# A two-layer attention network and two expert layers on one core: the order of the first transfers, the order of the first norms, and ten blank products

## The chip, the cores and the metric

The kernel runs on one core of one Trainium2 chip. The metric is the device time of one execution in microseconds (us); less is better. A core has TensorE (PE in the profile; PEld is its loading of weights), VectorE (DVE), ScalarE (ACT), GpSimd (POOL) and SyncE (SP). Each engine works through its own list of instructions in order and waits on semaphores for the others. Transfers are issued here by SP and, a few, by ACT; they run on 16 DMA engines that both queues share.

## The reference, cut to what matters

256 tokens of width 1024 pass through a first block of two layers (each with its own attention and an attention to 256 memory tokens) and then through a second block of two layers with three kinds of attention and 16 experts. The change touches only the beginning of the first layer:

```python
h = rmsnorm(x, norm_g[0])                    # rows x rsqrt(mean square) x a gain for each column
mem_h = rmsnorm(mem, mem_norm_g[0])
proj = einsum('bsd,de->bse', h, w_in_a[0])   # q, k, v of 24 heads, memory query, gate
kv = einsum('bnd,de->bne', mem_h, w_kv)      # keys and values of the memory, 4 heads
k = rmsnorm(k_of(kv), mem_kn_g[0])           # norm of each memory key over its 128 numbers
o_mem = softmax(q_mem @ k.T) @ v_of(kv)
```

## The kernel before, in words

**Products.** All large products are made from pairs of float32r numbers. A weight is cut into a high part (ACT, line 440) and what is left of it (DVE, line 448), and an activation likewise; a product is then three TensorE instructions (lines 507 to 509: high with high, low weight with high, high with low). The weights are walked in *quarters* of 256 rows of a 512-column slab: quarter q goes through ring buffer, ACT's cut, DVE's cut and TensorE's step q. A step is 2 token tiles x 2 blocks of 128 rows x 3 instructions = 12 products of 512 columns. Five cut quarters can be held at once (`NQ`), so ACT's cut of quarter q waits for TensorE's step q - 5.

**The first steps.** Steps 0 to 3 make the memory's keys (slab `mk0`), steps 4 to 7 its values (`mv0`); step 8 is the first quarter of `a00`, the first projection of the layer's own rows. The activations are not transposed on the chip: `mem_turned` and `x_turned` come turned from memory, ACT multiplies them by the norm's gain column by column and rounds to the high part (`act_gain_high`, line 697), DVE makes the low part (`dve_gain_low`, line 704). The row factors of the norm (`act_rows_norm`, line 730, and `dve_rows_factor`) are applied later, when ACT moves a finished product out of its bank (`act_proj_out`, line 575).

**The order around the change** is written out by hand in `act_layer_a`, `dve_layer_a`, `pe_layer_a` and `sp_first`:

- ACT issues two small transfers (`act_first_loads`): `gcol`, the gain columns (48 numbers on each of 128 partitions), and the first part of `const`, which holds the identity matrix. Both count on the semaphore `d_id`, and ACT and DVE begin with a wait for both (32).
- ACT then makes mhT (the memory's rows) with the cuts of quarters 0 to 2 between its pairs, cuts quarter 3, squares `mem_rows`, cuts quarters 4, 5 and 6 and moves `mk0` out; then come the norm of the memory keys (`act_head_norm`: squares at line 751, quarter 7, a root, quarter 8), and after it the eight instructions of hT (the layer's own rows), quarters 9 and 10, and so on.
- DVE follows the same order: `dve_head_norm` is quarter 7, the sum at line 763, the root (717 to 721), quarter 8, a multiplication (766), quarter 9, and the gain (771), which also needs `rows`; then the eight low parts of hT.
- TensorE does steps 0 to 8, turns the normed memory keys (`pe_flip`, line 656), and goes on with step 9.
- SP issues, in this order: half of `mem_turned`, half of the first ring load, the other half of `mem_turned`, ring loads to 2, `mem_rows`, ring load 3, `rows` (gains of the head norms), `x_turned`, ring load 4, `x_rows`, ring load 5, the rest of `const`. A ring load past the third waits until the buffer's last quarter has been cut by DVE.

Of the kernel before, what the change touches and what calls it, by code (L numbers as in the profile page):

```python
# [125 lines left out]
def program(nc, t, out, cols, keep):  # L126
# [14 lines left out]
    def sb(name, *shape, at=None, dt=F32):  # L141
        size = 4
        for n in shape[1:]:
            size *= n
        if at is None:
            place[name] = top_of[0]
            top_of[0] += (size + 63) // 64 * 64
        else:
            place[name] = place[at[0]] + at[1]
        return nc.alloc_sbuf_tensor_at(name, list(shape), dt, offset=place[name])  # L150

    def sem(name):
        return ctx.enter_context(nc.semaphore(name))
# [47 lines left out]
    maskR = sb("maskR", P, 2, TOK, dt=F32R)  # L201
    identR = sb("identR", P, P, dt=F32R)
    zeroR = sb("zeroR", P, 1, dt=F32R)
    squares = sb("squares", P, D, at=("S", 0))
    middle = [sb("middle0", P, D, at=("S", 4096)), sb("middle1", P, D, at=("PT", 0))]
    mem_rows = sb("mem_rows", P, 2, D, at=("PT", 0))
# [66 lines left out]
    def R(name):  # L273
        a, b = row_at[name]
        return rows[:, a:b]
# [102 lines left out]
    w_landed = [sem(f"w_landed{i}") for i in range(NR)]  # L378
    w_high, w_low, w_used = sem("w_high"), sem("w_low"), sem("w_used")
    d_id, d_const, d_rows, d_x, d_out = sem("d_id"), sem("d_const"), sem("d_rows"), sem("d_x"), sem("d_out")  # L380
    d_x0, d_x_turned, d_mem_rows, d_first = sem("d_x0"), sem("d_x_turned"), sem("d_mem_rows"), sem("d_first")


    first_normed, first_turned, second_normed = sem("first_normed"), sem("first_turned"), sem("second_normed")
# [15 lines left out]
    def write(pe, act, dve, pool, sp, branch):  # L400
# [12 lines left out]
        def sp_load(until):  # L413
            while sp.q < min(until, len(halves)):
                h = sp.q
                sp.q += 1
                view, srcs = halves[h]
                i = ring_of[h]
                if ring_before[h] >= 0:
                    sp.wait_ge((w_low, 2 * ring_before[h] + 2))  # L420
                for l in range(2):
                    if i >= NS and more_places[l][0] <= h < more_places[l][0] + NR:
                        sp.wait_ge(at("kS", l, 0))
                dst, a = view(ring[i]), 0
                if h == 0:
                    sp.e.dma_start(dst[:, 2:4, :], srcs[0][:, 2:4, :]).then_inc(w_landed[i], 16)
                    continue
                for src in srcs:
                    n = src.shape[2]
                    sp.e.dma_start(dst[:, :, a:a + n], src).then_inc(w_landed[i], 16)  # L430
                    a += n
# [146 lines left out]
        def kept(name):  # L578
            return at("kept", name, 1)
# [146 lines left out]
        def act_rows_norm(key, src, sq, *ready):  # L726
            ss = small(2, "ss", *key)
            for i in range(2):
                act.wait_ge(ready[min(i, len(ready) - 1)])
                act.e.activation(sq[:, i, :], src[:, i, :], SQUARE, accum_out=ss[:, i:i + 1]).then_inc(*act.did("sum", *key))  # L730
            act_root(key, ss, 2, 1.0 / D, "eps6")
# [7 lines left out]
        def dve_rows_factor(key):  # L739
            dve.wait_ge(at("sum", *key))  # L740
            dve_root(key, small(2, "ss", *key), 2, 1.0 / D, "eps6", factor(key))
# [344 lines left out]
        def sp_first():  # L1086
            quarter = 2 * TOK * 2

            def mem_half(n):
                sp.e.dma_start(mem_turned[:, 4 * n:4 * n + 4, :], t["mem_turned"][:, quarter * n:quarter * (n + 1)].rearrange("p (k n) -> p k n", k=4)).then_inc(d_mem[n], 16)  # L1090

            mem_half(0)
            view, srcs = halves[0]
            sp.e.dma_start(view(ring[ring_of[0]])[:, 0:2, :], srcs[0][:, 0:2, :]).then_inc(d_first, 16)
            mem_half(1)
            sp_load(3)
            sp.e.dma_start(mem_rows[:, :, :], t["mem"][0].rearrange("(t p) d -> p t d", p=P)).then_inc(d_mem_rows, 16)
            sp_load(4)
            sp.e.dma_start(rows[:, 0:t["rows"].shape[1]], t["rows"]).then_inc(d_rows, 16)
            sp.e.dma_start(x_turned[:, :, :], t["x_turned"].rearrange("p (k n) -> p k n", k=8)).then_inc(d_x_turned, 16)  # L1100
            sp_load(5)
            sp.e.dma_start(x_rows[:, :, :], t["x_rows"].rearrange("p (t d) -> p t d", t=2)).then_inc(d_x0, 16)
            sp_load(6)
            sp.e.dma_start(const[:, keep:t["const"].shape[1]], t["const"][:, keep:]).then_inc(d_const, 16)
            sp_load(8)
            sp.e.dma_start(X[:, :, :], t["x"][0].rearrange("(t p) d -> p t d", p=P)).then_inc(d_x, 16)
            sp_load((start("o00") + 14) // 2)
            sp.wait_ge(at("values", ("A", 5, 1)))
            for n in range(2):
                mem_half(n)  # L1110

        def act_first_loads():
            act.e.dma_start(gcol[:, :], t["columns"]).then_inc(d_id, 16)
            act.e.dma_start(const[:, 0:keep], t["const"][:, 0:keep]).then_inc(d_id, 16)

        def act_late_loads():
            act.wait_ge(at("tables", "cB"))
# [21 lines left out]
        LINE = [("a12", "g00"), ("a22", "g01"), ("a32", None), ("a42", None), ("a52", "g02"), (None, None)]  # L1139

        def pe_layer_a():
            pe_upto("a02")
            pe_ahead(9)
            pe.wait_ge((d_id, 32))
            pe_flip(("mKT", 0), chunk(qkv[1][1]), 4, [at("heads", "mk", 0)])
            pe_to("a02")
            for u in range(6):
                first, more = LINE[u]
                if first:
                    pe_upto(first)  # L1150
                pe_head_norm()
                if u == 5:
                    pe_ahead(1)
                    pe_gated("o0", 0, OUT_ORDER)
                    pe_upto("o00", 4)
                    pe_ahead(2)
                else:
                    pe_head_norm()
                pe_flip(("qT", u), chunk(qkv[u % 2][0]), 4, [at("heads", "q", u)])
                pe_ahead(2 if u == 5 else 3)  # L1160
                pe_flip(("kT", u), chunk(qkv[u % 2][1]), 4, [at("heads", "k", u)])
                units = group_units(u)
                if more:
                    pe_upto(more)
                if u == 4:
                    pe_to("mq0")
                    pe_head_norm(rope=False)

                    def between(n):
                        if n == 1:  # L1170
                            pe_flip(("qTm", 0), chunk(qkv[0][0]), 4, [at("heads", "mq", 0)])
                        pe_ahead(1 - n % 2)

                    pe_run(units + mem_units(0), between)
                    pe_to("a52")
                elif u == 5:
                    pe_gated("o0", 2, OUT_ORDER)
                    pe_upto("o00", 8)
                    pe_run(units, lambda n: pe_ahead(1 if n in (0, 2, 3) else 0))
                    pe_ahead(1)  # L1180
                    pe_gated("o0", 1, OUT_ORDER)
                    pe_upto("o00", 12)
                else:
                    pe_run(units, lambda n: pe_ahead(1 - n % 2))
                    pe_to(first)

        def act_layer_a():
            act.wait_ge((d_id, 32))
            act_gain_high(("mhT", 0), mem_turned, mhT[0], gcol[:, 16:24], [(d_mem[0], 16), (d_mem[1], 16)], lambda j0: act_cut(j0 // 2))
            act_upto("mv0")  # L1190
            act_ahead(1)
            act_rows_norm(("mem", 0), mem_rows, mem_rows, (d_mem_rows, 16))
            act_ahead(3)
            act_upto("a02")
            act_head_norm(("mk", 0), qkv[1][1], kept("mk0"), [], rope=False)
            act_gain_high(("hT", "A"), x_turned, hT[0], gcol[:, 0:8], [(d_x_turned, 16)] * 2)
            act_ahead(2)
            act_rows_norm(("x", 0), x_rows, mem_rows, (d_x0, 16))
            act_ahead(1)
# [60 lines left out]
                    act_to(first)  # L1260

        def dve_layer_a():
            dve.wait_ge((d_id, 32))
            dve.e.tensor_copy(identR[:, :], ident).then_inc(*dve.did())
            dve.e.tensor_scalar(zeroR[:, :], ident[:, 0:1], 0.0, None, MUL).then_inc(*dve.did("identR"))
            dve_gain_low(("mhT", 0), mem_turned, mhT, gcol[:, 16:24], lambda j0: dve_cut(j0 // 2))
            dve_upto("mv0")
            dve_ahead(1)
            dve_rows_factor(("mem", 0))
            dve_ahead(3)  # L1270
            dve_upto("a02")
            dve_head_norm(("mk", 0), qkv[1][1], gain=R("mk0"), amid=lambda: dve_ahead(1))
            dve_gain_low(("hT", "A"), x_turned, hT, gcol[:, 0:8])
            dve_ahead(1)
            dve_rows_factor(("x", 0))
            dve_ahead(1)
# [1241 lines left out]

            branch(l, lambda: way("few", (dve_few, act_few, pe_few)), lambda: way("all", (dve_all, act_all, pe_all)))

        act_first_loads()
        sp_first()
        dve_layer_a()
        dve_layer_b()
# [65 lines left out]
```

## Time and profile before

| | us |
|---|---|
| median of 3 runs | 1124.66 (1122.42 to 1126.36) |
| the profiled execution | 1124.96 |
| its span, first to last instruction | 1123.6 |
| PE busy | 1063.6 (95%) |
| DVE busy | 885.9 (79%) |
| ACT busy | 743.1 (66%) |

The span is what the profile's records cover; the profiled execution's own time is 1.36 us longer. The granted TensorE clock was 0.982 of full speed on average. "Idle before" in a timeline row stands in square brackets, with what ended it.

### The profile page before, as it was taken

The page shows a single profiled execution, that of the slowest core. Times are in us where ns is not written, and L with a number is a line of the kernel's source. Part 1 is how long each engine was busy: PE and PEld are TensorE (multiplying, and loading weights), DVE is VectorE, ACT ScalarE, POOL GpSimd, SP SyncE. Part 2 cuts the span into 40 slices and gives each one's busy share as a digit, 9 for nine tenths or more (in the row PEclk, how much of TensorE's full clock was granted, in tenths as well). Part 3 has the DMA queues.
Part 4 walks back from the last instruction along what each step waited for, and adds up shares of the span by engine and source line. Part 5 has one row for each costly group of instructions (what it writes and reads, how often), then busy time and mean ns, then how long its engine had stood idle before and what let it go on. Part 6 is the DMA issues. An engine that isn't in the chain of part 4 may idle for free.

```text
span 1123.6 us, 14563 instructions
## 1 busy us (share of the span) xinstructions
PE 1063.6 (95%) x5466; PEld 917.0 (82%) x5466; DVE 885.9 (79%) x1472; ACT 743.1 (66%) x1318; POOL 0.2 (0%) x4
## 2 busy tenths in 40 slices
PE   6899999999998999999999999999989999999996
PEld 5788888888787888888978788888878878788885
DVE  5756857777768867767588779999976877899996
ACT  6646665655666666486555457998845646699993
POOL 0000000000000000000000000000000000000000
PEclk9899999999999999999999899999999989999998
DMA  9754455443433645725542417999936332499991
GB/s 356 270 185 148 150 188 173 160 154 113 159 141 114 212 164 186 237 75 171 170 148 76 150 65 228 364 368 376 344 106 212 113 113 76 151 364 369 384 377 42
DMA packets 131283, 223.36 MB, mean 199 GB/s; under 512 B 6016, under 2 KB 76416, under 8 KB 130944
## 3 DMA queue, kind: packets, MB, share of 16 engines
q1 hardware_dynamic: 127312, 215.31, 55.3%
q10 hardware_dynamic: 3888, 6.98, 2.0%
q8 instruction: 47, 0.77, 0.3%
q14 instruction: 36, 0.29, 0.1%
HBM read 221.23 MB, written 1.05 MB: 198 GB/s over the span
## 4 chain that ended last, share of the span: by engine, by line
PE 48%; DVE 32%; ACT 11%; issue 6%; DMA 1%; SPq 0%; ACTq 0%; DVEq 0%
DVE wL L448 14%; PE bank L507 12%; PE bank L508 11%; PE bank L509 11%; ACT wH L440 4%; PE bank L886 3%; PE bank L822 3%; DVE sm L763 1%; PE bank L871 1%; DVE qkv L766 1%; ACT S L845 1%; DMA mem_rows<-in_mem 1%; PE bank L2302 1%; DVE mx L833 1%; DVE ys L2469 1%
## 5 line engine op out<-in xcount | busy, mean ns | idle before, releaser
L448 DVE TENSOR_TENSOR wL<-ring,wH 128x1024 fp32r<-128x1024 f32 (+1 forms) x316 | 375.3, 1212 | 122.7 <-ACT wH L440 121.9
L440 ACT ACTIVATE wH<-ring 128x1024 fp32r<-128x1024 f32 (+1 forms) x316 | 319.8, 1045 | 24.3 <-PE bank L509 16.3
L507 PE MATMUL bank<-wH,hTH 128*128 128x512 f32 (+2 forms) x592 | 231.2, 391 | 8.8 <-DVE hTL L704 4.4
L508 PE MATMUL bank<-wL,hTH 128*128 128x512 f32 (+2 forms) x592 | 224.3, 379 | 0.0
L509 PE MATMUL bank<-wH,hTL 128*128 128x512 f32 (+2 forms) x592 | 224.1, 379 | 0.0
L507 PEld LDWEIGHTS bank<-wH,hTH 128*128 128x128 f32 x592 | 113.3, 191 | 26.8 <-DVE wL L448 7.3
L509 PEld LDWEIGHTS bank<-wH,hTL 128*128 128x128 f32 x592 | 113.2, 191 | 14.5
L508 PEld LDWEIGHTS bank<-wL,hTH 128*128 128x128 f32 x592 | 113.5, 192 | 13.4 <-issue 0.5
L507 PE MATMUL bank<-wH,xgH 128*128 128x512 f32 x256 | 102.0, 398 | 2.5 <-DVE wL L448 2.3
L508 PE MATMUL bank<-wL,xgH 128*128 128x512 f32 x256 | 97.5, 381 | 0.0
L509 PE MATMUL bank<-wH,xgL 128*128 128x512 f32 x256 | 97.5, 381 | 0.0
L845 ACT ACTIVATE S<-bank,sm 128x256 f32<-128x256 f32 (+1 forms) x144 | 59.7, 428 | 45.0 <-DVE sm L837 42.7
L507 PEld LDWEIGHTS bank<-wH,xgH 128*128 128x128 f32 x256 | 48.8, 191 | 14.6 <-DVE wL L448 7.3
L877 ACT ACTIVATE PT<-bank 128x512 f32<-128x512 f32 x56 | 31.2, 597 | 41.1 <-PE bank L871 41.1
L509 PEld LDWEIGHTS bank<-wH,xgL 128*128 128x128 f32 x256 | 48.7, 190 | 7.0
L508 PEld LDWEIGHTS bank<-wL,xgH 128*128 128x128 f32 x256 | 48.9, 191 | 5.3
L575 ACT ACTIVATE qkv<-bank,factors 128x512 f32<-128x512 f32 x50 | 33.0, 688 | 27.0 <-PE bank L509 27.0
L448 DVE TENSOR_TENSOR wL<-ring_G,wH 128x1024 fp32r<-128x1024 f32 x40 | 48.4, 1218 | 1.0 <-ACT wH L440 1.0
L507 PE MATMUL bank<-wH,gh 128*128 128x512 f32 x128 | 49.0, 383 | 0.0
L448 DVE TENSOR_TENSOR wL<-ring_K,wH 128x1024 fp32r<-128x1024 f32 x40 | 48.2, 1219 | 0.8 <-ACT wH L440 0.7
L508 PE MATMUL bank<-wL,gh 128*128 128x512 f32 x128 | 48.5, 379 | 0.0
L509 PE MATMUL bank<-wH,gh 128*128 128x512 f32 x128 | 48.5, 379 | 0.0
(291 smaller groups left out, 1842.6 us busy)
## 6 DMA issues: line engine op xcount, KB each, us to landing
ring<-in_w_in_a SPq DMA_DIRECT2D x44, 1024.0 KB, 5.1
ring<-in_w_out SPq DMA_DIRECT2D x20, 1024.0 KB, 4.9
ring<-in_w_down SPq DMA_DIRECT2D x20, 1024.0 KB, 7.2
ring<-in_w_gate SPq DMA_DIRECT2D x36, 512.0 KB, 5.6
ring<-in_w_up SPq DMA_DIRECT2D x36, 512.0 KB, 7.2
ring<-in_w_in_b SPq DMA_DIRECT2D x14, 1024.0 KB, 5.2
ring<-in_w_in SPq DMA_DIRECT2D x8, 1024.0 KB, 5.2
ring<-in_w_mem_kv SPq DMA_DIRECT2D x7, 1024.0 KB, 7.2
```

The lines of the kernel that those rows point to most:

```text
L440: act.e.activation(quarter_parts(q)[0], quarter_in_ring(q), COPY).then_inc(w_high, 1)
L448: dve.e.tensor_tensor(lo, quarter_in_ring(q), hi.bitcast(F32), SUB).then_inc(w_low, 1)
L507: pe.e.matmul(o, a[0], high, start=first, stop=False)
L508: pe.e.matmul(o, a[0], low, start=False, stop=False)
L509: return pe.e.matmul(o, a[1], high, start=False, stop=last)
L575: act.e.activation(two_halves(dst(i)), from_woven(bank_of["proj", name, i].t, slab_w[name]), COPY, scale=factor(key)[:, i:i + 1] if key el ...
L763: dve.follow().tensor_reduce(ss.rearrange("p (t h) -> p t h", t=2), sq.rearrange("p t (h d) -> p t h d", d=P), AX, ADD).then_inc(*dve.did( ...
L766: dve.follow().tensor_tensor(v, v, bc(r.rearrange("p (t h) -> p t h", t=2).unsqueeze(3), [P, 2, n, P]), MUL).then_inc(*dve.did())
L822: mm = pe.e.matmul(score_bank(u, s // each)[:, s % each, :], u.qh(s)[:, i * P:(i + 1) * P], u.kh(s)[:, k:k + n], start=u.mask is None, sto ...
L845: act.e.activation(u.S[:, s, 0:n], score_bank(u, s // each)[:, s % each, :], EXP, bias=nb[:, s:s + 1], scale=u.scale, accum_out=u.den[:, s ...
L877: act.e.activation(u.PT[:, kt, :, :].rearrange("p h q -> p (h q)"), bank_of["turn", u.name, kt].t[:, :], COPY).then_inc(*act.did("PT", u.n ...
L886: mm = pe.e.matmul(b.t[:, s * u.dv:(s + 1) * u.dv], u.PT[:, kt, s, :], u.vh(s, kt), start=kt + s == 0, stop=kt == u.nk - 1, skip_group_che ...
```

## The change

1. SP issues `gcol` first of all, on a semaphore of its own (`d_columns`). The first part of `const` goes to SP too, behind ring load 2 and ahead of `mem_rows`, and counts alone on `d_id` (16). ACT issues neither. `x_turned` is issued ahead of ring load 4 as before, and `rows`, which stood ahead of `x_turned`, now comes behind ring load 4.
2. ACT begins with a wait for `d_columns`, and waits for `d_id` only ahead of the squares of `mem_rows`; DVE makes `identR` and `zeroR` there too.
3. On ACT and DVE the eight instructions of hT move ahead of the norm of the memory keys.
4. DVE first clears a new column, `blank`, and TensorE begins with ten products of it with itself, 512 columns each, in plain float32.

```diff
@@ program
+    blank = sb("blank", P, 1)
@@ sp_first
+            sp.e.dma_start(gcol[:, :], t["columns"]).then_inc(d_columns, 16)
             mem_half(0)
             view, srcs = halves[0]
             sp.e.dma_start(view(ring[ring_of[0]])[:, 0:2, :], srcs[0][:, 0:2, :]).then_inc(d_first, 16)
             mem_half(1)
             sp_load(3)
+            sp.e.dma_start(const[:, 0:keep], t["const"][:, 0:keep]).then_inc(d_id, 16)
             sp.e.dma_start(mem_rows[:, :, :], ...).then_inc(d_mem_rows, 16)
             sp_load(4)
-            sp.e.dma_start(rows[:, 0:t["rows"].shape[1]], t["rows"]).then_inc(d_rows, 16)
             sp.e.dma_start(x_turned[:, :, :], ...).then_inc(d_x_turned, 16)
             sp_load(5)
+            sp.e.dma_start(rows[:, 0:t["rows"].shape[1]], t["rows"]).then_inc(d_rows, 16)
             sp.e.dma_start(x_rows[:, :, :], ...).then_inc(d_x0, 16)
-        def act_first_loads():
-            act.e.dma_start(gcol[:, :], t["columns"]).then_inc(d_id, 16)
-            act.e.dma_start(const[:, 0:keep], t["const"][:, 0:keep]).then_inc(d_id, 16)
@@ pe_layer_a
+            pe.wait_ge(at("blank"))
+            b = att_bank(("idle", "first"), None)
+            for _ in range(10):
+                pe.e.matmul(b.t[:, :], blank[:, 0:1].to_broadcast([P, P]), bc(blank[:, 0:1], [P, 512]), start=True, stop=True)
             pe_upto("a02")
             pe_ahead(9)
-            pe.wait_ge((d_id, 32))
+            pe.wait_ge((d_id, 16))
@@ act_layer_a
-            act.wait_ge((d_id, 32))
+            act.wait_ge((d_columns, 16))
             act_gain_high(("mhT", 0), ...)
             act_upto("mv0")
             act_ahead(1)
+            act.wait_ge((d_id, 16))
             act_rows_norm(("mem", 0), mem_rows, mem_rows, (d_mem_rows, 16))
             act_ahead(3)
             act_upto("a02")
+            act_gain_high(("hT", "A"), x_turned, hT[0], gcol[:, 0:8], [(d_x_turned, 16)] * 2)
             act_head_norm(("mk", 0), qkv[1][1], kept("mk0"), [], rope=False)
-            act_gain_high(("hT", "A"), x_turned, hT[0], gcol[:, 0:8], [(d_x_turned, 16)] * 2)
             act_ahead(2)
@@ dve_layer_a
-            dve.wait_ge((d_id, 32))
-            dve.e.tensor_copy(identR[:, :], ident).then_inc(*dve.did())
-            dve.e.tensor_scalar(zeroR[:, :], ident[:, 0:1], 0.0, None, MUL).then_inc(*dve.did("identR"))
+            dve.e.memset(blank[:, :], 0.0).then_inc(*dve.did("blank"))
             dve_gain_low(("mhT", 0), ...)
             dve_upto("mv0")
             dve_ahead(1)
+            dve.wait_ge((d_id, 16))
+            dve.e.tensor_copy(identR[:, :], ident).then_inc(*dve.did())
+            dve.e.tensor_scalar(zeroR[:, :], ident[:, 0:1], 0.0, None, MUL).then_inc(*dve.did("identR"))
             dve_rows_factor(("mem", 0))
             dve_ahead(3)
             dve_upto("a02")
+            dve_gain_low(("hT", "A"), x_turned, hT, gcol[:, 0:8])
             dve_head_norm(("mk", 0), qkv[1][1], gain=R("mk0"), amid=lambda: dve_ahead(1))
-            dve_gain_low(("hT", "A"), x_turned, hT, gcol[:, 0:8])
             dve_ahead(1)
```

## Rows read from the trace of the kernel before

**Rows 1.** Page, part 4: shares of the whole span's chain by engine.

```profile
PE 48%; DVE 32%; ACT 11%; issue 6%; DMA 1%; SPq 0%; ACTq 0%; DVEq 0%
```

**Rows 2.** Waits of PE, 0 to 80 us: total, times, longest.

```profile
PE bank L507 <- DVE wL L448: 10.1, 1, 10.1
PE bank L507 <- DVE hTL L704: 4.4, 1, 4.4
```

**Rows 3.** Windows: length, busy PE, PEld, DVE, ACT, POOL, clock, DMA share, GB/s.

```profile
10.00:15.00 5.00, 4.94 (x12) 3.96 (x13) 4.18 (x8) 4.13 (x7) 0.00 (x0) 1.00 1.06 397
15.00:33.40 18.40, 18.40 (x86) 15.84 (x84) 11.32 (x18) 13.52 (x25) 0.00 (x0) 1.00 1.04 412
37.80:42.30 4.50, 4.46 (x11) 3.58 (x12) 4.32 (x12) 2.33 (x5) 0.00 (x0) 0.50 1.03 405
44.00:72.00 28.00, 28.00 (x131) 24.52 (x130) 13.99 (x15) 14.82 (x17) 0.00 (x0) 1.00 0.66 224
```

**Rows 4.** Chain of waits, 0 to 80 us: start, length, what.

```profile
4.26 13.39 DMA mem_rows<-in_mem
...
24.45 1.06 ACT T L751
...
30.37 3.20 ACT hTH L697 x8
...
35.69 1.22 DVE qkv L771
...
42.88 0.87 PE bank L656 x8
```

**Rows 5.** Timeline of ACT, the first waits: start, length, operation.

```profile
6.89 0.91 ACT L697 ACTIVATE mhTH<-mem_turned,gcol 128x256 fp32r<-128x256 f32 x2 [4.88 <-DMA const<-in_const]
17.68 1.06 ACT L730 ACTIVATE mem_rows<-mem_rows 128x1024 f32<-128x1024 f32 x1 [2.33 <-DMA mem_rows<-in_mem]
```

**Rows 6.** Timeline of DVE, 26 to 36 us: cuts of quarters 7, 8, 9.

```profile
26.49 1.23 DVE L448 TENSOR_TENSOR wL<-ring,wH 128x1024 fp32r<-128x1024 f32 x1 [1.58 <-ACT wH L440]
...
30.40 1.23 DVE L448 TENSOR_TENSOR wL<-ring,wH 128x1024 fp32r<-128x1024 f32 x1 [0.38 <-ACT wH L440]
...
34.54 1.23 DVE L448 TENSOR_TENSOR wL<-ring,wH 128x1024 fp32r<-128x1024 f32 x1 [1.78 <-ACT wH L440]
```

**Rows 7.** DMA issues: queue, size, us from issue to landing.

```profile
x_turned<-in_x_turned SPq DMA_DIRECT2D x1, 1024.0 KB, 11.6
rows<-in_rows SPq DMA_DIRECT2D x1, 776.0 KB, 9.7
```

**Rows 8.** Timeline of the issuing queues: start and length of an issue.

```profile
0.76 0.39 ACTq L1113 DMA_DIRECT2D gcol<-in_columns  x1
...
13.11 0.43 SPq L1100 DMA_DIRECT2D x_turned<-in_x_turned  x1
```

**Rows 9.** Windows of the first transfers; last number GB/s.

```profile
4.00:6.00 2.00, 0.00 (x0) 0.00 (x0) 0.00 (x0) 0.00 (x0) 0.00 (x0) 1.00 0.83 224
6.00:8.00 2.00, 0.00 (x0) 0.00 (x0) 0.46 (x3) 1.11 (x3) 0.00 (x0) 1.00 1.04 413
```

**Rows 10.** Timeline of PE: two plain float32 products of 512 columns.

```profile
860.07 1.88 PE L1763 MATMUL bank<-wukv,mKT 128*128 128x512 f32 x4
```

**Rows 11.** Timeline of PE and windows (PE busy, clock): products with a zero column.

```profile
666.02 2.87 PE L516 MATMUL bank<-zeroR,identR 128*128 128x512 f32 x12
...
664.00:668.00 4.00, 4.00 (x28) 1.00 0.01 2
```

**Rows 12.** Timeline of PE and the windows around it: short gaps, clock after.

```profile
624.86 0.66 PE L975 MATMUL bank<-const,Y 128*128 128x128 f32 x4 [1.23 <-DVE Y L893]
...
626.00:632.00 6.00, 6.00 (x16) 0.50 1.02 330
...
370.77 0.45 PE L507 MATMUL bank<-wH,yTH 128*128 128x512 f32 x1 [1.07 <-DVE yTL L992]
...
371.00:374.00 3.00, 3.00 (x15) 1.00 0.75 289
```

More of the change, by code:

```diff
@@ L380, in program @@
     d_id, d_const, d_rows, d_x, d_out = sem("d_id"), sem("d_const"), sem("d_rows"), sem("d_x"), sem("d_out")
-    d_x0, d_x_turned, d_mem_rows, d_first = sem("d_x0"), sem("d_x_turned"), sem("d_mem_rows"), sem("d_first")
+    d_x0, d_x_turned, d_mem_rows, d_first, d_columns = sem("d_x0"), sem("d_x_turned"), sem("d_mem_rows"), sem("d_first"), sem("d_columns")
     first_normed, first_turned, second_normed = sem("first_normed"), sem("first_turned"), sem("second_normed")
@@ L2519, in experts @@
             branch(l, lambda: way("few", (dve_few, act_few, pe_few)), lambda: way("all", (dve_all, act_all, pe_all)))
-        act_first_loads()
         sp_first()
```

## The prediction, made before the change was built or run

> **What bounds the kernel now.** I read the page first, for whether one engine sets the end. Over the whole span the chain runs through PE, DVE and ACT, and DMA has 1% of it [rows 1]. So nothing with a clock of its own (a stream of transfers that fills the whole time) sets the end, and time won early should reach the end.
>
> Then PE's waits in the first 80 us, where the change lies. There are two: 10.1 us for the first cut weight, and 4.4 us for hTL, the low part of the layer's own rows [rows 2]. The windows show what each costs beyond its length. From 10 to 15 us, 12 products take 4.94 us, 0.41 to 0.43 each; from 15 to 33.4 us, 86 take 18.40 us, 0.214 each; after the second wait 11 take 4.46 us again, at a granted clock of 0.50, the lower of the two levels, 1.2 GHz [rows 3]. (Ahead of 15 us the column shows 1.00 where the pace of the products says 0.5.) From 44 to 72 us PE is busy 28.00 of 28.00 us [rows 3]: from step 9 on it is PE alone that counts. So the number that I want is when step 9 starts. Before, that is 42.88 + 0.87 = 43.75 us, the end of turning the memory keys [rows 4].
>
> Last, the chain up to there: it is not PE. mem_rows lands at 4.26 + 13.39 = 17.65 us, ACT squares it (idle 2.33 us for it [rows 5]), cuts three quarters and moves `mk0` out until 24.45; then come the squares of the key norm at 24.45, hT on ACT for 3.20 us from 30.37, the end of the key norm on DVE at 35.69 + 1.22 = 36.91, then hTL [rows 4].
>
> **The change part by part.**
>
> *hT ahead of the key norm.* ACT's eight hT instructions now stand where the squares stood, at 24.45, and take 3.20 us [rows 4]: the squares begin at 27.65. From the squares to the end of the key norm it took 36.91 - 24.45 = 12.46 us. In these DVE stood idle 1.78 us for the cut of quarter 9, which ACT reached only after hT [rows 6]. That goes: without hT between, quarter 9 is cut right behind quarter 8, some 2 us before DVE asks for it. What is left is 10.68 us, so the keys are normed at 27.65 + 10.68 = 38.33 us, 1.4 us *later* than before. DVE's own low parts of hT follow ACT's pair by pair and are done at about 28.5, ahead of quarter 7: no cost.
>
> PE then turns the keys in 0.87 us [rows 4], behind a hand-over that I put at 0.15 us (an estimate; from mem_rows' landing to ACT it was 0.03 [rows 4, 5]). Step 9 starts at 38.33 + 0.15 + 0.87 = 39.35 instead of 43.75: **4.40 us** earlier. The gain is that step 8, at the lower clock from 37.8 us on [rows 3], no longer stands between the key norm and the turn; it lies ahead of it.
>
> What is late next on PE: quarter 7's cut ended 3.27 us behind the squares and quarter 8's 7.18 us behind them (26.49 + 1.23 and 30.40 + 1.23 less 24.45 [rows 6]), so they now end at 30.9 and 34.8. PE will be done with step 6 at 12.0 + 7 x 12 x 0.214 = 30.0 (the 12.0 is worked out below): a gap of 0.9 us, step 7 until 33.5, a gap of 1.3 us, step 8 until 37.4, a gap of 1.1 us for the keys. They are in the sum already, because step 9 is counted from the keys and not from PE.
>
> *The transfers.* x_turned landed at 13.11 + 11.6 = 24.71 us [rows 7, 8]; hT is now wanted at 24.45. `rows` (776 KB) moves from ahead of it to behind it, which at 412 GB/s [rows 3] is 1.9 us: 22.8, 1.6 us of cover. If it were gone, each us late would cost one. `rows` itself now queues behind ring load 4 and lands at about 27.4; it is wanted by the last multiplication of the key norm at 37.1. `x_rows` and later loads have the same bytes ahead of them as before.
>
> gcol's issue (0.39 us [rows 8]) now stands ahead of all of SP's. That is one end: everything 0.39 us later, mem_rows too. The other: between 4 and 6 us the engines move 224 GB/s, with the two small transfers in flight beside mem_turned on the second queue, and 413 GB/s from 6 on [rows 9]; the 2 us lose 2 x (413 - 224) / 413 = 0.92 us, and as much again may be lost from 2 to 4, where the start is in it too. If all came back, mem_rows would land 1.84 - 0.39 = 1.4 us earlier. The bytes and the small pieces still have to be carried, so I take 0.92 - 0.39, less a little: **0.4 us**, with -0.4 and 1.4 as ends. As ACT waits for mem_rows and the chain goes through that wait [rows 4, 5], this adds to the gain in full.
>
> The row above says that two queues at once cost throughput here. The Trainium skill, "DMA: Bandwidth & Descriptors", section "Issuing engines are not separate DMA queues", says that transfers of all issuers interleave on the same 16 engines and that issuing from several engines saves only the sequencer's time. By it, taking ACT's two issues to SP wins nothing on the wire and costs the issue: -0.4, and the whole gain would be 4.0 us instead of 4.8.
>
> *The waits.* ACT's first instruction waited until 6.89 for `const` [rows 5]; it may now go when gcol and the first half of mem_turned are there, 1 to 2 us earlier. That is worth nothing by itself, since ACT waits 2.33 us for mem_rows behind it. Nor does the new wait for `const` ahead of the squares cost: it is queued in front of mem_rows. DVE's two instructions for `identR` and `zeroR` (below 0.5 us together) now lie where DVE waits for ACT's squares anyway.
>
> *The ten blank products.* The nearest row of plain float32 at 512 columns is the one of the second block: two products give four records, 1.88 us in all [rows 10], 0.43 from start to start. So a product is two records, 0.86 us at full clock and 1.71 at half. PE can start at about 1.0 us, behind one small DVE instruction. All at full clock: 8.6 us, free at 9.6. All at half: 17.1 us, free at 18.1. Taken: half for the 4.9 us that the first products of before took (10.1 to 15.0 [rows 2, 3]), 5.7 records, then 14.3 records of 0.43 us: free at 12.0. That is 2 us *later* than the 10.1 at which real products begin now, at full pace from there. Steps 0 to 3 then end at 12.0 + 48 x 0.214 = 22.3, against 15.0 + 36 x 0.214 = 22.7 before: 0.4 us, and even this is hidden, since ACT's own chain is done with moving `mk0` out only at 24.45 - 0.4 [rows 4]. With about 0.6 us for the last half of that move (an estimate), the blanks become a cost once they end after 13; I take **0**, between 0 and the rival below.
>
> Sum: 4.40 + 0.4 = **4.8 us**. Own time of the profiled execution: 1124.96 - 4.8 = 1120.2; it lies 0.3 us above the median of the runs, so the median becomes 1124.66 - 4.8 = **1119.9 us**.
>
> **The rivals.**
>
> *The clock falls again in the gaps.* Three gaps of 0.9, 1.3 and 1.1 us within 8 us replace one of 4.4. For it: a gap of 1.23 us, ended at 624.9, was followed by a clock of 0.50 from 626 on [rows 12]. Against: one of 1.07 us was followed by 1.00 [rows 12], and here 12 dense products lie between gaps. Price: as after the second wait before, 11 products at 0.41 instead of 0.214 us, 2.2 us [rows 3]. Gain 2.6, median 1122.1. The trace has both outcomes for short gaps. The Trainium skill, "TensorE: Matmul & The Clock Gate", section "A second HAM failure mode: psum-queue depth-cycling", speaks for this rival: short idles between groups of products made the clock go back and forth; by it the time is this rival's.
>
> *Blanks that do not count (the other side).* If products of zeros leave the clock low, the blanks end at 18.1, the first real products run at half for another 4.9 us, and `mk0` ends at 18.1 + 4.9 + (48 - 12) x 0.214 = 30.7. ACT has moved it out at 31.3 instead of 24.45, and hT, which stands behind it on ACT, and the whole chain move by 6.9: step 9 starts at 39.35 + 6.9 = 46.2, **2.5 us later** than before, median 1127.2. It decides once the blanks end after about 17.5, where the 4.4 us are used up. For it: they are the only new work ahead of PE's real products. Against: products of a zero column ran at a clock of 1.00 from 664 to 668 us, 12 in 2.87 us [rows 11], though the clock was high before them.
>
> *The gain is given back later.* A later gap grows by what was won. For it: 95% busy PE leaves other waits. Against: after step 9 PE is full for 28 us and later transfers are released by cut quarters, so they move along. Median 1124.7.
>
> **How the numbers follow.** About 0.3% (3.4 us) is what a measurement of this kernel can tell from no change. Chances: forecast 0.63, clock 0.17, given back 0.11, blanks 0.06, other 0.03. The first, at 4.8 with ends 4.0 and 5.8, stays beyond 3.4 us nearly always, the second mostly not: faster 0.61, same 0.33, slower 0.06. Low end: 5.8 us and a little of the 2 us by which runs differ, 1117.6; high end: past the clock's rival, 1123.6.
>
> **What would show it.** PE's first products are 20 records that end near 12 us, the later ones at 0.214 us. No wait of PE above 2 us between 12 and 72 us. hT on ACT starts at 24.0, the key norm ends near 37.9, step 9 starts near 39.0, with PE full behind it. mem_rows lands near 17.3. The prediction is wrong if step 9 starts after 41, if a window from 33 to 42 us shows a clock near 0.50, or if the gain seen at step 9 is not there at the end.

## The result, and the profile after

The changed kernel took 1120.74 us (median of 10 runs, 1114.85 to 1123.68) beside 1125.69 us for the kernel before (10 runs): a ratio of 0.9948, 95% interval [0.9936, 0.9959], or 5.9 us less. (The quotient of the two medians alone is 0.9956, 4.95 us; the ratios with intervals are used from here on.) Measured twice more, beside other experiments, it came to 0.9954 [0.9936, 0.9972] and 0.9969 [0.9954, 0.9983]; the mean of the three is 0.9957, 4.8 us. The profiled execution took 1123.5 us, its span is 1122.2.

The waits of PE in the first 80 us (engine, what it waited for: total, times, longest), to be read beside [rows 2]:

```profile
PE bank L508 <- DVE wL L449: 1.9, 2, 1.1
PE bank L1144 <- DVE blank L1267: 0.9, 1, 0.9
PE bank L657 <- DVE qkv L772: 0.6, 1, 0.6
```

Of 14.5 us, 3.4 are left, and 0.9 of these is the wait before the first blank. (A line number behind the new column is one higher than before, further down five.) The chain of waits up to there (start, length, what), beside [rows 4]:

```profile
6.32 11.74 DMA mem_rows<-in_mem
...
24.89 3.19 ACT hTH L698 x8
28.08 0.95 ACT T L752
...
37.32 1.23 DVE qkv L772
38.69 1.06 PE bank L657 x8
39.75 0.22 PE bank L508
```

hT stands where the key norm's squares stood, the key norm ends at 38.55 instead of 36.91, later than before, and still the step behind the turn of the keys starts at 39.75 instead of 43.75. Nothing of step 8 lies between the two any more. PE's timeline shows the blanks and the waits that are left:

```profile
0.91 11.07 PE L1144 MATMUL bank<-blank 128*128 128x512 f32 x20 [0.91 <-DVE blank L1267]
11.41 0.78 PE L508 MATMUL bank<-wH,mhTH 128*128 128x512 f32 x1
...
35.19 0.48 PE L508 MATMUL bank<-wH,hTH 128*128 128x512 f32 x1 [1.05 <-DVE wL L449]
...
38.69 1.06 PE L657 MATMUL bank<-const,qkv 128*128 128x128 f32 x8 [0.64 <-DVE qkv L772]
...
39.51 0.46 PE L508 MATMUL bank<-wH,hTH 128*128 128x512 f32 x1
```

In this view step 9 starts at 39.51 (before: 43.51); the table below uses this one. The windows of the changed kernel (columns as in [rows 3]) show two things: the clock stays at 1.00 through the short gaps from 33 to 42 us, and PE is full from 44 to 72 us, as before.

```profile
4.00:6.00 2.00, 2.00 (x4) 0.73 (x3) 0.00 (x0) 0.16 (x1) 0.00 (x0) 1.00 0.83 225
6.00:8.00 2.00, 2.00 (x6) 0.82 (x5) 0.88 (x2) 1.35 (x3) 0.00 (x0) 1.00 1.01 386
33.00:42.00 9.00, 7.31 (x38) 5.90 (x37) 8.25 (x14) 8.94 (x15) 0.00 (x0) 1.00 0.80 294
44.00:72.00 28.00, 28.00 (x132) 24.57 (x131) 13.76 (x13) 14.34 (x17) 0.00 (x0) 1.00 0.65 230
```

How far does the 4.0 us reach? One wait of PE that both kernels have lies in the attention at 360 us. In the kernel before:

```profile
363.71 2.08 PE L886 MATMUL bank<-qkv,PT 128*128 128x128 f32 x8 [2.84 <-ACT PT L877]
```

and in the changed kernel:

```profile
359.72 1.55 PE L887 MATMUL bank<-qkv,PT 128*128 128x128 f32 x8 [2.84 <-ACT PT L878]
```

It comes 3.99 us earlier: all that step 9 won is still there. But at 625 us the lead is gone: the products that begin at 624.86 in [rows 12] begin here at 625.21, and in the third measurement of the same changed kernel, whose profiled span was 1117.8, at 620.87, 3.99 us earlier than before:

```profile
625.21 0.65 PE L976 MATMUL bank<-const,Y 128*128 128x128 f32 x4
...
620.87 0.66 PE L976 MATMUL bank<-const,Y 128*128 128x128 f32 x4 [1.23 <-DVE Y L894]
```

Between lies a stretch in which the granted clock of the first of these two executions was low although PE was full. It fell among three short waits of PE, 0.41, 0.40 and 0.20 us, of which these are the last two:

```profile
602.48 0.54 PE L1845 MATMUL bank<-const,G 128*128 128x128 f32 x2 [0.40 <-DVE G L1697]
603.22 1.12 PE L976 MATMUL bank<-const,Y 128*128 128x128 f32 x4 [0.20 <-DVE Y L894]
```

The other execution has the same three waits (0.41, 0.38 and 0.30 us), and its clock stayed up. The windows of the changed kernel (PE alone: busy, clock, DMA share, GB/s):

```profile
600.00:604.00 4.00, 3.32 (x23) 0.83 0.36 144
604.00:616.00 12.00, 12.00 (x34) 0.50 0.00 1
```

of the kernel before:

```profile
604.00:616.00 12.00, 11.29 (x68) 1.00 0.06 24
```

and of the changed kernel in its third measurement:

```profile
604.00:616.00 12.00, 12.00 (x70) 1.00 0.00 1
```

34 records of products in 12 us against 70: this stretch costs one execution some 6 us, and another execution of the same kernel nothing. The kernel before has its own at 626 us [rows 12], by which part of the lead comes back, and the span ends 1.4 us shorter. So one profiled span can't judge this change; the start of step 9 and the ratio over many runs can.

### The profile page after: what moved, and what is told of

It reads as the page before. It is cut to its first block, busy times and chain, and to the rows that moved or that the text cites. A ratio compares the mean times of both kernels' runs of the same rounds, so it can differ in the third digit from the quotient of the medians.

```text
span 1122.2 us, 14604 instructions
## 1 busy us (share of the span) xinstructions
PE 1075.3 (96%) x5486; PEld 923.2 (82%) x5486; DVE 886.3 (79%) x1473; ACT 743.1 (66%) x1318; POOL 0.2 (0%) x4
## 3 DMA queue, kind: packets, MB, share of 16 engines
HBM read 221.23 MB, written 1.05 MB: 198 GB/s over the span
## 4 chain that ended last, share of the span: by engine, by line
PE 50%; DVE 31%; ACT 11%; issue 5%; DMA 1%; SPq 0%; ACTq 0%; DVEq 0%
DVE wL L449 14%; PE bank L508 12%; PE bank L509 11%; PE bank L510 11%; ACT wH L441 4%; PE bank L887 3%; PE bank L823 3%; PE bank L872 2%; DVE sm L764 1%; DVE qkv L767 1%; ACT S L846 1%; PE bank L2307 1%; DMA mem_rows<-in_mem 1%; DVE ys L2474 1%; DVE T L2490 1%
```

## The experiments

"Step 9" is its first product in PE's timeline; ratios are to the kernel before on the same chip.

| kernel | step 9, us | ratio, 95% interval |
|---|---|---|
| before | 43.51 | 1 |
| changed, three times | 39.51, 39.39, 39.40 | 0.9948, 0.9954, 0.9969 |
| the move of hT alone | 39.41 | 0.9974 [0.9963, 0.9986] |
| the transfers alone | 43.35 | 1.0002 [0.9992, 1.0012] |
| changed without blanks | 39.50 | 0.9975 [0.9964, 0.9986] |
| the same again | 39.34 | 0.9966 [0.9952, 0.9979] |
| changed, 20 blanks | 47.02 | 1.0033 [1.0023, 1.0043] |
| the move and the blanks | 39.47 | 0.9955 [0.9938, 0.9973] |
| | step 10, us | |
| changed | 42.18 | as above |
| keys turned behind step 9 | 41.24 | 0.9960 [0.9945, 0.9975] |
| cuts 7 and 8 ahead of hT | 39.84 | 0.9956 [0.9940, 0.9971] |
| the same again | 39.84 | 0.9940 [0.9929, 0.9952] |
| the same without blanks | 39.88 | 0.9941 [0.9927, 0.9955] |

**The move alone** (kernel before, one edit on ACT and the same on DVE):

```diff
+            act_gain_high(("hT", "A"), x_turned, hT[0], gcol[:, 0:8], [(d_x_turned, 16)] * 2)
             act_head_norm(("mk", 0), qkv[1][1], kept("mk0"), [], rope=False)
-            act_gain_high(("hT", "A"), x_turned, hT[0], gcol[:, 0:8], [(d_x_turned, 16)] * 2)
```

> Kernel before with one edit: hT ahead of the norm of the memory keys on ACT and DVE; transfers as before, no blank products. Theory A (the order of the two norms is the whole gain): hT on ACT starts at 24.7 (x_turned lands there, 24.45 was the squares' place), the key norm ends near 38.5, step 9 starts at 39.4 to 39.7 instead of 43.75, and the time is 4.0 to 4.4 us below the kernel before, the same as the changed kernel within 1 us. Theory B (PE's early start at full clock is the gain) and theory C (the order of the transfers is): step 9 stays within 1 us of 43.75 and the time within 1 us of before.

Measured: 0.9974, 2.9 us less (1.6 to 4.2), and step 9 at 39.41. Its timeline of ACT has hT start at the landing of x_turned:

```profile
24.66 3.31 ACT L697 ACTIVATE hTH<-x_turned,gcol 128x256 fp32r<-128x256 f32 x8 [0.30 <-DMA x_turned<-in_x_turned]
```

The move alone puts step 9 where the whole change puts it. Theories B (PE's early start) and C (the order of the transfers) fall for that stretch. The `rows` transfer behind x_turned saves this wait of 0.30 us and no more; in the whole change the later landing of mem_rows, 0.4 us, takes it back.

**The transfers alone** (the changed kernel's transfers and semaphores, hT behind the key norm, no blanks):

```diff
-            act_gain_high(("hT", "A"), x_turned, hT[0], gcol[:, 0:8], [(d_x_turned, 16)] * 2)
             act_head_norm(("mk", 0), qkv[1][1], kept("mk0"), [], rope=False)
+            act_gain_high(("hT", "A"), x_turned, hT[0], gcol[:, 0:8], [(d_x_turned, 16)] * 2)
```

> Kernel before with the changed kernel's transfers and semaphores alone: no blank products, hT behind the key norm as before. Theory A: ACT's first instruction runs a us earlier, but mem_rows lands 0.4 us later (18.06 as in the changed kernel), and step 9 starts at 44.2, 0.4 us later than before; time 0 to 0.5 us above before. Theory C: step 9 starts near 40 and the time is 4 to 5 us below before.

Measured: 1.0002, no change. The wait for hTL is back in PE's timeline:

```profile
38.21 0.45 PE L508 MATMUL bank<-wH,hTH 128*128 128x512 f32 x1 [4.52 <-DVE hTL L705]
```

mem_rows landed at 6.41 + 11.55 = 17.96 us, 0.3 later than before, and PE's step 8 started 0.4 later, as expected. Step 9 still came 0.16 us earlier than before, where 0.4 us later was expected. In this execution the clock fell later: the first products of step 8 still follow each other at 0.22 us, and only from 39.18 on at 0.43 us. In the kernel before all but the end of step 8 ran at 0.50 [rows 3]. PE's timeline, and the window (PE alone: busy, clock, DMA share, GB/s):

```profile
38.72 0.38 PE L510 MATMUL bank<-wH,hTL 128*128 128x512 f32 x1
...
39.18 0.63 PE L509 MATMUL bank<-wL,hTH 128*128 128x512 f32 x1
...
38.00:43.00 5.00, 4.79 (x17) 0.66 1.01 392
```

**Without the blanks**:

```diff
-            pe.wait_ge(at("blank"))
-            b = att_bank(("idle", "first"), None)
-            for _ in range(10):
-                pe.e.matmul(b.t[:, :], blank[:, 0:1].to_broadcast([P, P]), bc(blank[:, 0:1], [P, 512]), start=True, stop=True)
```

> Changed kernel without the ten blank products. Theory A: PE starts real products at 9.8, 12 of them at 0.41 us, ends the memory keys at about 22.5 (22.9 with the blanks), hT starts at 24.9 as in the changed kernel, step 9 starts at 39.5, and the time is that of the changed kernel within 0.5 us. Theory B: the lower clock comes back at the start and costs 2 us or more at step 9 and at the end.

Measured: step 9 at 39.50, as with the blanks, but the time 0.9975, 3.0 us above the changed kernel's first ratio, not within the 0.5 expected. Two readings were open: the blanks win 2 to 3 us behind 72 us, or the difference lies in the clock of later stretches. The mean granted clock of the runs differs too: 0.985 over the ten of the changed kernel, 0.981 over these eight.

**Twenty blanks**:

```diff
-            for _ in range(10):
+            for _ in range(20):
```

> Changed kernel with twenty blank products instead of ten. Theory A with the limit that the prediction worked out (blanks cost once they end after 13): they end at 11.5 + 10 x 0.86 = 20.1, the memory keys end at 30.4, hT starts at 31.1, step 9 at 45.6, 6 us later than in the changed kernel; time 6 us above it, 1 to 2 us above the kernel before. Rival (PE's start is free, as ACT and DVE carry the chain): no change.

Measured: 1.0033, 3.7 us above before, and step 9 at 47.02, 7.5 us behind the changed kernel. 6 were expected: the blanks were to end at 20.1 and ended at 0.91 + 20.39 = 21.30, 1.2 us later. ACT's timeline shows the price where the prediction put it: its cuts and the move out of `mk0` wait for PE, and hT stands behind.

```profile
23.93 1.06 ACT L441 ACTIVATE wH<-ring 128x1024 fp32r<-128x1024 f32 x1 [2.07 <-PE bank L510]
...
30.40 0.69 ACT L576 ACTIVATE qkv<-bank,factors 128x512 f32<-128x512 f32 x1 [2.77 <-PE bank L510]
...
32.28 3.29 ACT L698 ACTIVATE hTH<-x_turned,gcol 128x256 fp32r<-128x256 f32 x8
```

**The changed kernel again, and the move with the blanks** (kernel before, hT moved, the ten blanks added, transfers as before):

> The changed kernel, unchanged, once more. Step 9 of its trace and those of the kernels with the move alone and without the blanks all lie 4.0 to 4.1 us ahead of before, yet its time was 0.9948 of before and theirs 0.9974 and 0.9975. Theory A (the blanks do nothing past step 9; the 2 to 3 us between them are the clock of later stretches by chance): the ratio comes out at 0.9965 to 0.9978. Theory D (the blanks win 2 to 3 us somewhere behind 72 us): 0.994 to 0.9955 again.

> Kernel before with hT ahead of the key norm and the ten blank products; transfers as before. Theory A: step 9 at 39.4 as with the move alone, time as with the move alone (0.9974 of before, within 0.001). Theory D: 2 to 3 us below the move alone, near 0.995.

Measured: 0.9954 and 0.9955, which spoke for theory D. But the intervals are 0.0036 wide and overlap those without blanks, and no kernel with the ten blanks had been compared with one without on the same chip.

**The keys turned behind step 9**:

```diff
-            pe_ahead(9)
+            pe_ahead(10)
```

> Changed kernel with the turn of the memory keys behind step 9 instead of ahead of it. In the changed kernel TensorE waits 0.64 us for the key norm ahead of the turn. Theory A: that wait goes, step 10 starts at 41.4 instead of 42.1, 0.65 us earlier, and the time is 0.6 us below the changed kernel, which five rounds can't tell. Rival: ACT's copies of the turned keys come later too and hold the cuts of quarters 12 to 14, and step 12 starts no earlier.

Measured: the wait of 0.64 us is gone and step 10 starts at 41.24 (42.18 in the changed kernel), 0.9 us earlier; the ratio 0.9960 can't be told from the changed kernel's, as expected. The rival falls: PE goes on without a gap, and step 12 starts at 46.51 instead of 47.36.

**Cuts of quarters 7 and 8 ahead of hT** (and the turn behind step 9; the key norm on DVE then makes no cut ahead of its sum and none behind its root):

```diff
-            pe_ahead(9)
+            pe_ahead(10)
@@ act_layer_a
+            act_ahead(2)
             act_gain_high(("hT", "A"), ...)
             act_head_norm(("mk", 0), ...)
-            act_ahead(2)
@@ dve_layer_a
+            dve_ahead(2)
             dve_gain_low(("hT", "A"), ...)
-            dve_head_norm(("mk", 0), qkv[1][1], gain=R("mk0"), amid=lambda: dve_ahead(1))
+            dve_head_norm(("mk", 0), qkv[1][1], gain=R("mk0"), a=0, b=0, amid=lambda: dve_ahead(1))
```

> Changed kernel with the cuts of quarters 7 and 8 ahead of hT on ACT and DVE (the key norm then cuts 9 and 10 where it cut 7 and 8) and the turn of the keys behind step 9. If ACT's and DVE's chain is what TensorE waits for: steps 7 and 8 follow without a gap (0.4 and 1.05 us before), the key norm ends at 37.1, the turn lies at 38.7 and step 10 starts at 39.6 instead of 42.1, 2.5 us earlier; time 2.5 us below the changed kernel, about 0.994 of before or lower. Rival: TensorE's gaps only move to steps 9 and 10, and step 10 starts at 41 or later.

Measured: step 10 at 39.84, 2.3 us ahead of the changed kernel (2.5 expected); the ratio, 0.9956, showed none of it in six runs. So both this and the blanks were taken two by two on one chip:

> The changed kernel a third time, on one chip with the next three: two by two, with and without the ten blanks, with the cuts of quarters 7 and 8 behind and ahead of hT. Theory A (time follows the start of step 10, 42.1 us here, plus the low stretches of the clock behind it): 4.0 us below before, less up to 1 for later low stretches, ratio 0.9965 to 0.9973; within 1 us of the kernel without blanks. Theory D (the blanks win about 2 us at the end that no stretch ahead of 72 us shows): 0.995, 2 us below the kernel without blanks.

> Changed kernel without the blanks, again. Theory A: within 1 us of the changed kernel, ratio 0.9965 to 0.9975. Theory D: 2 us above it, 0.997 to 0.998.

> The early cuts (quarters 7 and 8 ahead of hT, turn of the keys behind step 9) without the blanks. Theory A: step 10 starts at 39.8 as with blanks, 2.3 us ahead of the changed kernel; time 2.3 us below the changed kernel without blanks, and within 1 us of the early cuts with blanks; ratio about 0.995. Theory D: 2 us above the early cuts with blanks.

> The early cuts with the blanks, again: the best of the four by both theories. Theory A: 2.3 us below the changed kernel, ratio about 0.995. Theory D: 0.993, since both gains add up. If neither (0.9956 as in its first measurement, equal to the changed kernel), what was won at step 10 is given back behind it.

Measured: changed 0.9969 with blanks and 0.9966 without; early cuts 0.9940 with and 0.9941 without. In both pairs the blanks make no difference (0.0003 and 0.0001, intervals of 0.0023 to 0.0029 on each ratio), and the early cuts win 0.0025 to 0.0029, about 3 us, in both. Theory D falls; an effect of the blanks below about 2 us, either way, isn't excluded. The clock goes with this: in the first pair the mean granted clock of the runs is 0.9825 with blanks and 0.9834 without, where it was 0.985 against 0.981 in the first comparison. The window of the early cuts without blanks shows why they win: PE, at 7.31 of 9.00 us in the changed kernel, is full.

```profile
33.00:42.00 9.00, 9.00 (x46) 1.00 0.94 340
```

This version and the second measurement of its twin with blanks have the lowest ratios of all, 0.9941 and 0.9940; the twin's first measurement, 0.9956, was no better than the changed kernel's beside it (0.9954).

All seven measurements of kernels with step 9 at 39.3 to 39.5 average 0.9963, 4.2 us; their step 9 lies 4.0 to 4.2 us earlier than before. The three with step 10 at 39.8 to 39.9 average 0.9946, 6.1 us; step 10 of the kernel before is at 46.18 in its timeline, 6.3 us later. Twenty blanks: 3.5 us later at step 9, 3.7 us at the end. What is won ahead of 44 us arrives whole, on average; a single ratio is known to 1 to 2 us only.

## Why the prediction was right, and where it was not

*hT ahead of the key norm: 4.40 us predicted.* Right. In the changed kernel hT starts 0.44 us later than its place in [rows 4] (24.89 against 24.45) and step 9 4.00 us earlier: 4.44 from the move itself. The move alone: hT 0.21 late, step 9 4.10 earlier: 4.31. The terms: from the squares to the end of the key norm 38.55 - 28.08 = 10.47 us (10.68 predicted), the turn of the keys 1.06 (0.87 predicted). That these two misses cancel is luck.

What the prediction names in one clause, that step 8 ran at the lower clock, is about half of the gain. The first and the last product of step 8 on PE, before and in the changed kernel:

```profile
37.84 0.77 PE L507 MATMUL bank<-wH,hTH 128*128 128x512 f32 x1 [4.37 <-DVE hTL L704]
...
42.50 0.38 PE L509 MATMUL bank<-wH,hTL 128*128 128x512 f32 x1
```

```profile
35.19 0.48 PE L508 MATMUL bank<-wH,hTH 128*128 128x512 f32 x1 [1.05 <-DVE wL L449]
...
37.67 0.38 PE L510 MATMUL bank<-wH,hTL 128*128 128x512 f32 x1
```

From first to last it took 4.66 us behind the wait of 4.37 us, at a clock of 0.50 [rows 3], and takes 2.48 us now, at 1.00. An estimate from these rows: at the full clock step 9 of the kernel before would have started 2.2 us earlier, and the move would have won some 1.8 us there.

*The transfers: 0.4 us gained, predicted.* Wrong in sign: mem_rows landed at 6.32 + 11.74 = 18.06 instead of 17.65, 0.4 us later. The step that failed is the one that laid the slow stretch of [rows 9] to the two small transfers in flight beside mem_turned. With both in SP's queue gcol had landed at 0.73 + 1.8 = 2.5 us, and `const`, queued behind the ring loads, landed at 4.42 + 11.2 = 15.6. The issues of the changed kernel on SP's queue (start, length), and from the DMA view (queue, size, us to landing):

```profile
0.73 0.39 SPq L1093 DMA_DIRECT2D gcol<-in_columns  x1
...
4.42 1.86 SPq L1099 DMA_DIRECT2D const<-in_const  x1
...
gcol<-in_columns SPq DMA_DIRECT2D x1, 24.0 KB, 1.8
...
const<-in_const SPq DMA_DIRECT2D x1, 67.0 KB, 11.2
```

And yet the engines moved 225 GB/s from 4 to 6 us (the window above), against 224 before. The delay has the size of gcol's issue, 0.39 us, which now stands ahead of all others; no run moved gcol by itself, so that this is its cause is argued, not shown. The Trainium skill, "DMA: Bandwidth & Descriptors", section "Issuing engines are not separate DMA queues", says that transfers of all issuers interleave on the same 16 engines. The trace agrees: 224 GB/s with the two transfers on ACT's queue, 225 with both on SP's. By that rule the prediction put the gain at 4.0 us, and step 9 starts 4.00 us earlier.

*ACT's first instruction 1 to 2 us earlier, worth nothing.* Right. The timeline of ACT, beside [rows 5]:

```profile
5.84 0.91 ACT L698 ACTIVATE mhTH<-mem_turned,gcol 128x256 fp32r<-128x256 f32 x2 [3.83 <-DMA mem_turned<-in_mem_turned]
...
18.14 1.06 ACT L731 ACTIVATE mem_rows<-mem_rows 128x1024 f32<-128x1024 f32 x1 [2.62 <-DMA mem_rows<-in_mem]
```

*The blanks: free at 12.0, worth 0.* Right: 0.91 + 11.07 = 11.98. Their weight loads in the changed kernel show the price of one and the place where the clock rose:

```profile
4.49 0.34 PEld L1144 LDWEIGHTS bank<-blank 128*128 128x128 f32 x1 [0.52 <-issue]
5.34 0.20 PEld L1144 LDWEIGHTS bank<-blank 128*128 128x128 f32 x1 [0.52 <-issue]
5.78 0.19 PEld L1144 LDWEIGHTS bank<-blank 128*128 128x128 f32 x1 [0.24 <-issue]
```

0.85 us from one record to the next until 5.34, 0.43 to 0.44 from there. That blanks which end late enough cost was shown with twenty of them: they end 9.3 us later than ten and step 9 starts 7.5 us later, so the cost begins at about 13.8 if it then grows one for one (an estimate; 13 was predicted, and no run ends its blanks between 12 and 21). The clock rose later there, at 6.9 us:

```profile
6.20 0.34 PEld L1144 LDWEIGHTS bank<-blank 128*128 128x128 f32 x1 [0.52 <-issue]
6.91 0.19 PEld L1144 LDWEIGHTS bank<-blank 128*128 128x128 f32 x1 [0.38 <-issue]
```

*What is late next on PE.* The gaps of 1.3 and 1.1 us were 1.05 and 0.64, and the one of 0.9 for quarter 7 is not among the waits. One that I had not seen, 0.8 us for quarter 4, is: PE is done with the memory's keys before ACT, late with mem_rows, has cut it. It costs nothing either.

*The rivals.* The clock did not fall in the gaps: it was 1.00 from 33 to 42 us, where it had been 0.50 behind the long wait [rows 3]. The Trainium skill, "TensorE: Matmul & The Clock Gate", section "A second HAM failure mode: psum-queue depth-cycling", tells of short idles between groups of products that made the clock go back and forth; this stretch does not show it. The rows at 602 us show that it can come out otherwise: there the clock fell among shorter waits in one execution and not in another. Blanks of zeros did raise the clock. And nothing is given back on average, though in a single execution the stretch from 604 to 616 us takes some 6 us, more than the change gives.

*The number.* 4.8 us predicted, 5.9 in the first measurement, 4.8 over three. By its terms it should have said 4.0, since one term had the wrong sign. That the mean of three ratios meets 4.8 is luck: step 9 shows 4.0 to 4.1 us in all three, and the seven measurements above average 4.2.

## What to carry to other kernels

Where one engine is full from some point on, find the instruction that opens this stretch and work back from it: here the order of work on two helper engines was worth 4 us, the order of the transfers and the main engine's early start nothing that could be measured. An item whose result is wanted late (the key norm) should not stand ahead of one that the main engine waits for first (hT), even if it then ends later itself. A long wait can cost more than its length: here the step behind 4.4 us of waiting lost 2.2 us more to the lower clock. And judge a gain of a few us by that instruction's start and by many runs, not by one profiled span.

## What the runs showed of the hardware that I had not expected

- The first transfers ran at 225 GB/s between 4 and 6 us, whether two small transfers lay beside them on a second queue or not, and at 386 GB/s (413 before) from 6 to 8 us. What holds them back was not settled.
- Products of zeros raised TensorE's clock: by their pace they ran at the lower level from 0.91 to 5.3 us and at the upper from there; in the run with twenty blanks the rise came at 6.9 us. Real products of the kernel before had it rise at 15 us, 4.9 us after their start [rows 2, 3].
- The low stretches of the clock in mid-kernel move and change their length between executions of one kernel: 0.50 from 604 to 616 us in one, 1.00 in another, and the same short waits (0.2 to 0.4 us) stand ahead of both. The ten runs of the changed kernel spread over 8.8 us, more than the edit is worth. Most of this goes with the clock: the mean granted clock was 0.980 in the two slowest runs (1123.50 and 1123.68) and 0.991 in the fastest (1114.85), and over the ten the correlation of time and clock is -0.90.
- Two long waits of PE ended differently: behind 4.37 us step 8 began at the lower level in the kernel before, and behind 4.52 us, with the transfers alone, it began at the upper level and fell to the lower 0.9 us later.
